# Sliding-window attention in half blocks of 64 queries and 192 keys, on quarter arrays of TensorE

## What is computed

```python
def _alibi_window_bias(diff, key_ok):
    valid = (diff >= 0) & (diff < WINDOW) & key_ok
    slopes = _alibi_slopes()[:, :, None, None]
    pen = -slopes * diff[..., None, None, :, :].astype(jnp.float32)
    return jnp.where(valid[..., None, None, :, :], pen, NEG_BIG)

def _sink_attention(q, k, v, bias, sinks):
    s = jnp.einsum('...qhgd,...khd->...hgqk', q, k).astype(jnp.float32) * (ATT_HEAD_DIM ** -0.5) + bias
    sink = jnp.broadcast_to(sinks.astype(jnp.float32)[:, :, None, None], s.shape[:-1] + (1,))
    p = jax.nn.softmax(jnp.concatenate([s, sink], axis=-1), axis=-1)[..., :-1]
    return jnp.einsum('...hgqk,...khd->...qhgd', p.astype(v.dtype), v)
```

## Time and profile before

| | |
|---|---|
| Runs of the kernel before | 596.15, 596.87, 598.35 us; median 596.87 |
| The profiled execution, its own time | 598.34 us |
| Its span in the profile | 596.5 us |
| Mean granted clock of TensorE over the span | 0.994 |
| Instructions in the profile | 9003 |

### The profile page before, as it was taken

How to read it: one execution, slowest core, us unless ns; L and a number is a source line. 1 busy time by engine, 2 the same in 40 slices (tenths; PEclk the granted TensorE clock), 3 DMA queues, 4 the chain that set the end, 5 groups by cost and what they waited for, 6 DMA issues and landing times.

```text
span 596.5 us, 9003 instructions
## 1 busy us (share of the span) xinstructions
PE 575.7 (97%) x3587; PEld 524.6 (88%) x3587; DVE 272.3 (46%) x536; ACT 208.3 (35%) x548; POOL 138.9 (23%) x145
## 2 busy tenths in 40 slices
PE   4999999998999999999999999999799999999996
PEld 4999999998888888889999898899799998888874
DVE  5620013663666666621376766534345545232323
ACT  6742212414444444430445454223323315021011
POOL 3000031023244334431021312034422221010001
PEclk9999999998999999999999999999999999999998
DMA  9752200621011010013013111411122324134231
GB/s 317 268 186 87 76 1 12 241 78 55 17 37 37 2 36 35 3 36 112 1 44 99 36 56 35 108 36 37 36 71 71 89 88 121 56 141 141 71 123 53
DMA packets 26433, 47.01 MB, mean 79 GB/s; under 512 B 3268, under 2 KB 17860, under 8 KB 26248
## 3 DMA queue, kind: packets, MB, share of 16 engines
q1 hardware_dynamic: 25960, 45.91, 23.7%
q10 hardware_dynamic: 432, 0.53, 0.2%
HBM read 39.40 MB, written 8.01 MB: 79 GB/s over the span
## 4 chain that ended last, share of the span: by engine, by line
PE 88%; ACT 3%; DVE 3%; POOL 3%; issue 2%; DMA 1%; DVEq 0%; ACTq 0%; POOLq 0%
PE ps L547 44%; PE ps L485 8%; PE ps L486 8%; PE ps L487 8%; PE ps L591 3%; PE ps L629 3%; PE ps L611 2%; POOL zaT L1573 2%; PE ps L698 1%; PE ps L732 1%; PE ps L676 1%; PE ps L710 1%; PE ps L490 1%; PE ps L489 1%; PE ps L700 1%
## 5 line engine op out<-in xcount | busy, mean ns | idle before, releaser
L547 PE MATMUL ps<-x_hl,w_hi 128*128 128x364 f32 (+1 forms) x1200 | 305.6, 334 | 12.8 <-ACT x_hl L824 6.5
L547 PEld LDWEIGHTS ps<-x_hl,w_hi 128*128 128x128 f32 x1200 | 212.5, 190 | 22.8 <-issue 7.1
L547 PE MATMUL ps<-x_hl,w_lo 128*128 128x364 f32 (+1 forms) x600 | 199.0, 332 | 0.0
L547 PEld LDWEIGHTS ps<-x_hl,w_lo 128*128 128x128 f32 x600 | 113.8, 190 | 0.1
L940 ACT ACTIVATE prob<-prob,nmx 128x256 f32<-128x256 f32 (+1 forms) x64 | 30.9, 485 | 56.6 <-DVE sd L1239 56.6
L1526 POOL TENSOR_TENSOR prob<-prob,rden 128x1024 f32<-128x1024 f32 (+1 forms) x16 | 28.6, 1789 | 74.2 <-DVE rden L1245 74.2
L328 POOL TENSOR_TENSOR w_lo<-w_raw,w_hi 128x1024 fp32r<-128x1024 f32 x13 | 32.5, 2498 | 47.7 <-ACT w_hi L863 47.7
L485 PE MATMUL ps<-wt_hi,x_hl 128*128 128x324 f32 x128 | 39.9, 312 | 0.0
L487 PE MATMUL ps<-wt_hi,x_hl 128*128 128x324 f32 x128 | 39.8, 311 | 0.0
L486 PE MATMUL ps<-wt_lo,x_hl 128*128 128x324 f32 x128 | 39.8, 311 | 0.0
L1576 POOL TENSOR_TENSOR qmT<-qmT,sg 128x364 f32<-128x364 f32 (+1 forms) x24 | 23.3, 973 | 66.1 <-DVE sg L1428 36.8
(11 more groups left out here) (229 smaller groups left out, 892.8 us busy)
## 6 DMA issues: line engine op xcount, KB each, us to landing
w_raw<-in_w_in_tiles SPq DMA_DIRECT2D x24, 512.0 KB, 3.6
x_tok<-in_x_prompt SPq DMA_DIRECT2D x8, 512.0 KB, 4.5
w_raw<-in_w_out_tiles SPq DMA_DIRECT2D x8, 512.0 KB, 3.6
x_res<-in_x_prompt SPq DMA_DIRECT2D x8, 512.0 KB, 4.1
out_y_prompt<-y_out SPq DMA_DIRECT2D x7, 512.0 KB, 2.9
wt_raw<-in_w_tok SPq DMA_DIRECT2D x4, 648.0 KB, 7.1
Cs<-in_state_C SPq DMA_DIRECT2D x8, 256.0 KB, 2.9
out_C_sample<-Cs SPq DMA_DIRECT2D x8, 256.0 KB, 2.4
```

Source lines behind the costliest of these rows:

```text
L547: last = mm(ps[:, sub_bank(sub), 0:w], wt, xm, start=(at_ == 0), stop=(at_ == 23))
```

## The change

Each block of 128 queries is taken as two halves of 64 (h = 0, 1), and each half meets the 192 keys that end with it. The half's queries lie on one half of the PSUM partitions.

- `scores`: eight products per unit where there were four, each with 64 rows, 64 queries as weights and 192 keys as moving columns. Head kv selects the row half of the array, h the column half.
- The score, exponential and normalising steps run over 192 keys per head instead of 256. Units 0 and 1 run over 128 as before; the first 64 of these have a bias table of their own, `bias_0`.
- `prob_transposes`: for each of four heads one transpose of 128 of its keys, starting at key 0 for g = 0 and at key 64 for g = 1, and for each pair of heads one transpose of the 128 columns that hold the last 64 keys of the one and the first 64 of the other. Six for eight. ACT then copies 256 columns where it copied 512.
- `values`: eight products with 128 keys, then eight with 64, all with 64 queries as moving columns. Group g = 0, 1 writes to bank 4 + g, for every unit, so the unit before must have been copied out: `att_out` is waited for one unit earlier.
- Where a stretch of keys starts in the middle of a token tile, the weights come from `va_sh`, a copy of `va` shifted by 64 tokens, which SP makes by two DMAs from SBUF to SBUF of 64 partitions by 8 tiles by 128 columns (256 KB each). It lies where the raw token-major weights lay.
- The bias table of the prompt has 192 columns per head for 256, and `bias_first` 64.

The core of the diff:

```diff
@@ -205,16 +207,18 @@
-    bias_p = sb("bias_p", [P, AH, 2 * WIN], F32, GI + 17408)
+    bias_p = sb("bias_p", [P, AH, KEYS_H], F32, GI + 17408)
+    bias_0 = sb("bias_0", [P, AH, HQ], F32, GI + 17408 + 4 * AH * KEYS_H)
+    va_sh = sb("va_sh", [P, NC + 1, KV_W], F32, Wr)
...
-    prob = sb("prob", [P, 2, G, 2 * WIN], F32, Fr)
+    prob = sb("prob", [P, 2, G, KEYS_H], F32, Fr)
@@ -390,7 +394,13 @@
+        sp.dma_start(bias_0[:], i["bias_first"]).then_inc(s("att_ld"), 16)
...
+        wait(sp, "wt_lo", 4)
+        wait(sp, "tok_act", NC)
+        wait(sp, "tok_dve", NC)
+        sp.dma_start(va_sh[0:HQ, 1:NC + 1, :], va[HQ:P, 0:NC, :]).then_inc(s("va_sh"), 16)
+        sp.dma_start(va_sh[HQ:P, 0:NC, :], va[0:HQ, 0:NC, :]).then_inc(s("va_sh"), 16)
@@ -584,13 +594,17 @@
             if u < 2 * NC:
                 blk, pair = u // 2, u % 2
-                k0 = 1 if blk == 0 else 0
                 for g in range(2):
-                    for kv in range(KVH):
-                        rows = slice(kv * HD, (kv + 1) * HD)
-                        last = mm(ps[:, kv, g * 256 + k0 * WIN:g * 256 + 256],
-                                  qaT[rows, 2 * pair + g, blk * P:(blk + 1) * P],
-                                  kaT[rows, (blk - 1 + k0) * P:(blk + 1) * P], start=True, stop=True)
+                    for h in range(2):
+                        for kv in range(KVH):
+                            rows = slice(kv * HD, (kv + 1) * HD)
+                            q0 = blk * P + h * HQ
+                            if blk == 0:
+                                keys = kaT[rows, 0:HQ].unsqueeze(1).broadcast_to([HD, 2, HQ]) if h == 0 else kaT[rows, 0:P]
+                            else:
+                                keys = kaT[rows, q0 - WIN:q0 + HQ]
+                            last = mm(ps[h * HQ:(h + 1) * HQ, kv, g * 256 + (HQ if blk == 0 else 0):g * 256 + KEYS_H],
+                                      qaT[rows, 2 * pair + g, q0:q0 + HQ], keys, start=True, stop=True)
             else:
@@ -605,11 +619,17 @@
-            if u < 2 * NC:
-                for kb in range(1 if u < 2 else 0, 2):
-                    for g in range(G):
-                        last = nc.tensor.transpose(ps[:, 2 + kb, g * P:(g + 1) * P],
-                                                   prob[:, u % 2, g, kb * WIN:(kb + 1) * WIN], ident[:])
+            if u < 2:
+                for g in range(G):
+                    last = nc.tensor.transpose(ps[:, 3, g * P:(g + 1) * P], prob[:, u % 2, g, HQ:KEYS_H], ident[:])
+            elif u < 2 * NC:
+                pr = prob[:, u % 2].rearrange("p g k -> p (g k)")
+                for g in range(G):
+                    k0 = KEYS_H * g + HQ * (g % 2)
+                    nc.tensor.transpose(ps[:, 2, g * P:(g + 1) * P], pr[:, k0:k0 + WIN], ident[:])
+                for kv in range(KVH):
+                    k0 = 2 * KEYS_H * kv + WIN
+                    last = nc.tensor.transpose(ps[:, 3, kv * P:(kv + 1) * P], pr[:, k0:k0 + 2 * HQ], ident[:])
             else:
@@ -620,15 +640,37 @@
         def values(u):
...
             wait(pe, "pT_dve", u - 1)
-            wait(pe, "att_out", u - 1)
+            wait(pe, "att_out", u)
             if u < 2 * NC:
...
-                for kb in range(1 if blk == 0 else 0, 2):
-                    for kv in range(KVH):
-                        rows = slice(kv * HD, (kv + 1) * HD)
-                        last = mm(ps[rows, 4 + u % 2, 0:2 * P], va[:, blk - 1 + kb, rows],
-                                  probT[:, u % 2, kb, kv * 2 * P:(kv + 1) * 2 * P],
-                                  start=(kb == 0 or blk == 0), stop=(kb == 1), skip_group_check=True)
+                if u == 0:
+                    pe.wait_ge(s("va_sh"), 32)
+
+                def head(g, rows, h):
+                    return ps[rows, 4 + g, h * HQ:(h + 1) * HQ]
+
+                if blk == 0:
+                    for h in range(2):
+                        for g in range(2):
+                            for kv in range(KVH):
+                                rows = slice(kv * HD, (kv + 1) * HD)
+                                part = slice(0 if h else HQ, P)
+                                last = mm(head(g, rows, h), (va[:, 0, rows] if h else va_sh[HQ:P, 0, rows]),
+                                          probT[part, u % 2, 1, (2 * kv + g) * P + h * HQ:(2 * kv + g) * P + (h + 1) * HQ],
+                                          start=True, stop=True, skip_group_check=True)
+                else:
+                    for g, h in ((0, 0), (0, 1), (1, 0), (1, 1)):
+                        v = va[:, blk - 1 + g] if g == h else va_sh[:, blk]
+                        for kv in range(KVH):
+                            rows, c0 = slice(kv * HD, (kv + 1) * HD), (2 * kv + g) * P + h * HQ
+                            mm(head(g, rows, h), v[:, rows], probT[:, u % 2, 0, c0:c0 + HQ], start=(h == 0), stop=False, skip_group_check=True)
+                    for h in range(2):
+                        for g in range(2):
+                            v = va[:, blk - g] if g == h else va_sh[:, blk + 1 - 2 * g]
+                            for kv in range(KVH):
+                                rows, half = slice(kv * HD, (kv + 1) * HD), slice(g * HQ, (g + 1) * HQ)
+                                last = mm(head(g, rows, h), v[half, rows], probT[half, u % 2, 1, kv * P + h * HQ:kv * P + (h + 1) * HQ],
+                                          start=False, stop=True, skip_group_check=True)
             else:
@@ -944,14 +986,15 @@
-            A_(probT[0:n, u % 2, 1, :], ps[0:n, 3, :], ACT.Copy).then_inc(s("pT_act"), 1)
+            cols = slice(0, 2 * P if 2 <= u < 2 * NC else G * P)
+            A_(probT[0:n, u % 2, 1, cols], ps[0:n, 3, cols], ACT.Copy).then_inc(s("pT_act"), 1)
...
         def out_evac(u):
...
             if u < 2 * NC:
                 blk, pair = u // 2, u % 2
...
-                   ps[:, 4 + u % 2, 0:2 * P].rearrange("p (g t) -> p g t", g=2), ACT.Copy)\
+                   ps[:, 4:6, 0:P], ACT.Copy)\
...
             else:
@@ -1217,14 +1260,17 @@
-                dve.wait_ge(s("att_ld"), 64)
+                dve.wait_ge(s("att_ld"), 80)
...
             if u < 2 * NC:
...
-                k0 = WIN if u < 2 else 0
-                p = prob[:, b, :, k0:]
-                step(STT(out=p, in0=ps[:, 0:2, :].rearrange("p b (g k) -> p (b g) k", g=2)[:, :, k0:], scalar=rstd_q[:, u // 2:u // 2 + 1],
-                         in1=bias_p[:, heads, k0:], op0=ALU.mult, op1=ALU.add))
+                p = prob[:, b, :, HQ if u < 2 else 0:]
+                raw = ps[:, 0:2, :].rearrange("p b (g k) -> p (b g) k", g=2)
+                parts = [(0, KEYS_H, bias_p)] if u >= 2 else [(HQ, WIN, bias_0), (WIN, KEYS_H, bias_p)]
+                for k0, k1, bias in parts:
+                    last = STT(out=prob[:, b, :, k0:k1], in0=raw[:, :, k0:k1], scalar=rstd_q[:, u // 2:u // 2 + 1],
+                               in1=bias[:, heads, :] if bias is bias_0 else bias[:, heads, k0:k1], op0=ALU.mult, op1=ALU.add)
+                step(last)
...
             else:
@@ -1605,8 +1651,9 @@
-    diff = tok[:, None, None] + WIN - np.arange(2 * WIN)[None, None, :]
+    diff = tok[:, None, None] % HQ + WIN - np.arange(KEYS_H)[None, None, :]
...
+    bias_first = np.where(tok[:, None, None] < HQ, f(NEG), bias_prompt[:, :, HQ:WIN])
```

More of the change, by code:

```diff
@@ L43 @@
 KEYS_S = WIN + DEC_T
+HQ = P // 2
+KEYS_H = WIN + HQ
 W1 = MD + 1
@@ L215, in build @@
     prob_s = sb("prob_s", [P, 4, KEYS_S], F32, Fr)
-    new_s = sb("new_s", [P, 4, T_S], F32, Fr + 2560)
-    k_out = sb("k_out", [P, 2, KV_W], F32, Fr + 4096)
+    new_s = sb("new_s", [P, 4, T_S], F32, Fr + 6144)
+    k_out = sb("k_out", [P, 2, KV_W], F32, Fr + 7168)
     mx = small("mx", [P, 2, 4])
@@ L936, in exps @@
             b = u % 2
-            k0 = WIN if u < 2 else 0
+            k0 = HQ if u < 2 else 0
             for g in range(4):
@@ L980, in g_exp @@
                 act.wait_ge(s("v_out"), 32)
-                act.wait_ge(s("att_ld"), 64)
+                act.wait_ge(s("att_ld"), 80)
                 A_(Gt[:, 0, 0:2, :].rearrange("p h t -> p (h t)"), ps[:, 0, 256:512], ACT.Exp).then_inc(s("g_done"), 1)
@@ L1523, in normalise @@
             if u < 2 * NC:
-                k0 = WIN if u < 2 else 0
+                k0 = HQ if u < 2 else 0
                 p = prob[:, b, :, k0:]
-                Q.tensor_tensor(p, p, rden[:, b, :].unsqueeze(2).broadcast_to([P, G, 2 * WIN - k0]), ALU.mult)\
+                Q.tensor_tensor(p, p, rden[:, b, :].unsqueeze(2).broadcast_to([P, G, KEYS_H - k0]), ALU.mult)\
                     .then_inc(s("prob_ready"), 1)
@@ L1626, in constants @@
             "seq_mask": np.where(same & (st[:, None] <= st[None, :]), f(-NEG), f(NEG)),
-            "bias_prompt": bias_prompt, "bias_sample": bias_sample, "resets": resets,
+            "bias_prompt": bias_prompt, "bias_first": bias_first, "bias_sample": bias_sample, "resets": resets,
```

## The result

| | before | change |
|---|---|---|
| Median of 7 runs each | 598.35 us | 592.94 us |
| Lowest and highest | 596.15, 598.53 | 589.86, 594.56 |
| Profiled execution | 598.34 us | 594.56 us |
| Its mean granted clock | 0.994 | 0.992 |

The ratio is 0.9912 (0.9886 to 0.9938), 5.4 us less on the medians. The forecast was 589.6 us, in a range from 587.0 to 594.0. The change is faster by more than 0.5%, by 5.4 us on the medians where 7.3 were forecast, about three quarters, and its runs are spread over 4.7 us. The forecast of 589.6 started from a median of 596.87 for the kernel before; in this comparison that median was 598.35, and the same -7.3 us counted from it gives 591.1.

What follows compares the result with a forecast made beforehand. PE's own work was taken to set the time in the attention stretches. Terms -9.0 (units 2 to 15), +0.3 (units 0 and 1) and +1.4 (DMA queue) sum to -7.3 us: 589.6 us from a median of 596.87, range 587.0 to 594.0.

Steps and rivals of the forecast that it cites:

- Attention blocks, -9.0 + 0.3: PE's transposes, values and scores: 0.64 us less in each of units 2 to 15, 0.3 more for units 0 and 1.
- Rival 4: Scores and second values, units 2 to 15: quarter arrays run only two at a time; +4.9 us, 601.8; chance 0.04.
- rival 5: PE's short value rounds pay on top of their columns, 0.086 for 0.058 us; 4.7 us, 594.3; chance 0.03.
- Unit 0's values: Values of units 0 and 1: four rounds on quarters and four on halves, 0.76 us, 0.18 more each.
- the join: Second values to scores on PE, units 2 to 15: no gap; gain 9.0 us with it, 6.8 without.
- Rival 2: No join: pipe empties between second values and scores, 14 x 0.16 = 2.2 us; 591.8, or 593.5 with the clock; chance 0.15.
- Other engines, nothing: Attention stage: shorter score, exponential, POOL and ACT copy work costed at nothing, since PE hides it.
- The DMA queue, +1.4: SP's two shifted copies ahead of weight tile 4 delay its landing and PE near 122 us: 512 KB at 371 GB/s.
- The upper bound, 2.8: DMA delay of weight tile 4 by the shifted copies: 2.8 us if read and write cost both.
- PE pays each further delay in full: PE's start on weight tile 4 near 122 us: every further delay of its landing delays PE equally, +1.4 us.
- The clock, rival 1: The longer wait at 122 us, 0.7 to 2.1, also drops PE's clock: 1.7 us, 591.3; chance 0.25.
- The forecast case: Whole kernel: all terms as summed, -7.3 us, 589.6 us against the median; chance 0.45.

Runs made afterwards that it cites:

- parts_swapped: Changed kernel with its value parts in the other order, 64-key products first, 128-key products second: 591.36 us, ratio 0.99.
- before_copies: Kernel before plus only the change's two SBUF-to-SBUF copies at the same place of SP's queue, data unused: 599.71 us, ratio 1.0034.
- tile4_first: Changed kernel with weight tile 4 loaded ahead of all attention loads and the shifted copies issued behind it: 589.52 us, ratio 0.9865.
- before_dram: Kernel before plus one unused 512 KB load from HBM in the place of the two SBUF-to-SBUF copies: 596.85 us, ratio 0.999.
- change_rows_early: Changed kernel, copies still ahead of tile 4, with exponentials of the gate rows made one sub-block earlier: 587.13 us, ratio 0.9814.
- the second: Second comparison: the changed kernel unaltered, run once more against the kernel before: 590.27 us, ratio 0.9891.
- copies_late: Changed kernel with its two shifted copies issued behind the load of weight tile 4, not ahead of the window copies: 588.84 us, ratio 0.9859.
- copies_late_again: copies_late run once more, unaltered, beside a rerun of the changed kernel: 590.32 us, ratio 0.9871.
- rows_early_first: tile4_first with exponentials of the gate rows made one sub-block earlier: 585.70 us, ratio 0.9802.
- rows_early_late: copies_late with exponentials of the gate rows made one sub-block earlier: 586.52 us, ratio 0.9815.

## Why the prediction was right and where it was wrong

**Attention blocks, -9.0 + 0.3: right to a twentieth.** 8.24 us measured for 8.7. Each of the four blocks is within 0.01 of its term. Two roads led there: counting from start to start, and reading the sample's blocks as prices for small tiles. Rival 4 (pairs) is refuted by the same rows, sixteen score records in 0.76 us where it asked for 1.41, and so is rival 5 (0.086 a round), by value parts of 0.62 and 0.28 where it asked for 0.83 and 0.39. The Trainium skill (TensorEngine Tiling, Instruction Overhead) gives each matmul some 60 cycles of overhead. As something added to each it does not show here: without their borders the first value part and the scores leave rounds of 0.059 and 0.164, for columns that need 0.054 and 0.161. Unit 0's values are also as summed, 159.91 to 160.67, 0.76.

**What is missing of it is the join, counted 14 times.** It needs values followed by scores of the prompt. PE's timeline at the last such place:

```profile
244.77 0.27 PE L672 MATMUL ps<-probT,va 64*64 64x64 f32 x2
...
245.17 0.69 PE L614 MATMUL ps<-kcT,qs 64*32 64x136 f32 x32
```

Here the second part takes 0.40 for 0.28, and the last two units are followed by a projection. Eleven units join, three pay, 3 x 0.16 = 0.5 us. The loop quoted ahead of the prediction says so (`if it < N_ATT`); I had taken a middle unit for all. Rival 2 itself did not come: in the change no gap stands between 64x64 blocks that meet, and parts_swapped shows the gap coming back at its forecast price.

**Other engines, nothing: right.** No wait of PE for probabilities or copies stands in the waits of the change.

**The DMA queue, +1.4: the term that failed.** I named the right transfer and the right engine. Two halves of the step were wrong. The price: "512 KB at 371 GB/s" took bytes for bytes, but the landing moved by 3.35 in the profiled execution, by 2.9 in before_copies, and by 0.9 for the same bytes from memory. The upper bound, 2.8 if read and write cost both, came nearer in the first two, though other executions of the copies show 1.7 and about 2. And "PE pays each further delay in full" was false in the other direction. POOL's 3.56 us of the earlier trace rows was not the split's own length. DVE's timeline of the kernel before in those microseconds, and POOL's in tile4_first, where it began together with another of DVE's scans:

```profile
118.26 2.25 DVE L1188 TENSOR_TENSOR_SCAN row<-row,row 4x1024 f32<-4x1024 f32 x1
120.45 3.25 DVE L1191 TENSOR_TENSOR_SCAN row<-row,m0T,row 4x8 f32<-4x8 f32 x8
```

```profile
115.92 2.39 POOL L332 TENSOR_TENSOR w_lo<-w_raw,w_hi 128x1024 fp32r<-128x1024 f32 x1 [10.79 <-ACT w_hi L905]
```

Unhindered the split takes 2.4. In the kernel before it stood behind DVE's scan until 120.4 and ended at 122.71. A tile that ACT can begin by about 119.2 (its 1.1 us, then POOL at 120.4) costs PE nothing, which before_dram shows; each microsecond after that costs one. Two traces bear this out: with landings of 119.70 (change_rows_early) and 120.91 (before_copies), 0.5 and 1.7 past that point, PE waits 1.01 and 2.21, which is 0.46 and 1.66 more than 0.55. In the change's first profile the landing at 121.36 leaves 2.16, and 0.67 come on top, since POOL's split (3.06 for 2.39) now met another row of DVE, the first of these two:

```profile
122.06 1.28 DVE L1242 TENSOR_TENSOR rows<-row,row 4x1088 f32<-4x1088 f32 x1
123.38 3.31 DVE L1243 TENSOR_TENSOR rows<-row,row 4x1088 f32<-4x1088 f32 x1
```

That makes the 2.83.

**The clock, rival 1, given 0.25: it came in both profiled executions of the change,** for 1.61 us at 125.69. Other executions were probably without it, though none of them was profiled: 594.71 less the 2.37 between waits of 3.38 and 1.01 and less two falls of 1.6 is 589.1, and 589.3 is the lowest that was measured. My reason against it, that 0.7 us of wait dropped nothing, was sound for 0.7 and said little of a wait whose length I had sized too small.

**The sum.** Forecast -8.7 + 1.4 = -7.3. In the profiled execution: -8.24 + 2.83 + 1.61 = -3.80. Over the runs the two last terms vary: -5.4 by the medians of the first comparison and -7.5 by those of the second (597.78 to 590.27). The forecast case is one that the change has in some executions and not in others. That the first median fell inside the range owes something to luck. The upper end of 594.0 was made of rivals 1 and 2. Rival 2 did not come, and its 2.2 us made room for a DMA term larger than summed and for a median of the kernel before that was 1.5 us higher; the profiled execution, 594.56, lies outside.

**Open:** why tile 4 lands at 119.7 in one execution and 121.7 in another with the same queue (the DMA records show the difference already in the window copies ahead of it, which end at 117.93 and 119.86); and what decides, after the same 2.2 us of waiting, whether the granted clock falls. One part of the change was not tried by itself, the second bias table.

## What to carry to other kernels

Count a saving at every place where it is made, the first and last rounds of a loop apart: a border between two blocks is there only where the two blocks meet. Before a kernel's new copies are priced, look at what stands behind them in the same queue and at what it must beat: here the order of a few lines cost up to 4.4 us in an execution, of the 8.2 that the change gains in its blocks, and with the gate rows early, putting the urgent load ahead of everything gave another 0.8 (585.70 for 586.52). A wait of PE of 2.2 us cost 3.8 here in some executions, by the fall of the clock after it; taking it away made the kernel faster and its times narrower, so that smaller effects can be measured at all.

## What was not expected of the hardware

**POOL and DVE held each other up.** In tile4_first POOL's split and a DVE scan began 0.05 us apart; POOL took its 2.39 and the scan 4.60 for 2.41:

```profile
115.97 4.60 DVE L1230 TENSOR_TENSOR_SCAN row<-resets,row 4x1088 f32<-4x1088 f32 x1
```

4.60 is the sum of the two less 0.2. In copies_late the scan came first and it was POOL that waited:

```profile
118.67 4.25 POOL L332 TENSOR_TENSOR w_lo<-w_raw,w_hi 128x1024 fp32r<-128x1024 f32 x1 [13.38 <-ACT w_hi L905]
```

DVE's eight small scans took 1.16 in the change and 3.25 in the kernel before, and in the change a product of 4 partitions took 3.31 for 1.28 (the two rows of DVE above). The Trainium skill (SBUF — State Buffer, Terms) says that the two engines share a pair of ports whose lock is held for a whole instruction, and that the loser "fully blocks"; these rows agree, with instructions of four partitions on one side. A long row of POOL or DVE beside the other's is thus no measure of its own length.

**Two copies from SBUF to SBUF weighed more than one load of the same bytes:** ahead of tile 4 512 KB moved its landing by 0.9 us from memory, in one trace, and by between 1.7 and 3.7 from SBUF, in five (119.70 to 121.67, against 118.01; without either it came between 117.53 and 118.57).

**The granted clock fell after the same wait in some executions and not in others.** After the wait of 2.22 us before scores(0) the stretch took 4.80 us at a granted 1.00 or 6.3 at 0.73, that is partly at 1.2 GHz for 2.4, in kernels that differ in nothing there: copies_late 4.80 above, and copies_late_again, the same program:

```profile
138.81:145.10 6.29, 6.29 (x40) 5.92 (x40) 2.30 (x8) 2.69 (x10) 1.18 (x2) 0.73 0.04 11
```

It fits the two levels of the kernel before, near 596.8 and 598.4: the profile at 598.34 has the fall, and that of before_dram at 596.70 has none. Of the nine traces with this wait six show the fall. After tile 4 it came after both waits of 3.38 and after none of 0.55, 1.01, 1.34 and 2.21.

A fall can also cost nothing. After another wait of PE, of 2.17 us near 409, the clock fell in rows_early_first and not in rows_early_late:

```profile
408.40:413.00 4.60, 4.60 (x18) 4.60 (x19) 1.73 (x2) 2.71 (x4) 1.60 (x2) 0.63 0.01 4
```

```profile
408.40:413.00 4.60, 3.92 (x23) 3.93 (x24) 2.36 (x4) 2.03 (x4) 0.98 (x1) 1.00 0.02 4
```

Yet rows_early_first is the faster of the two by 0.71 us (585.67 and 586.38 in the profiled executions), as much as its lead when that wait ended (408.39 against 409.07): PE at full clock waited again, 1.12 us at 418.43 and 0.20 at 422.89, and the slower PE did not. So a fall of the clock cost time where PE's own work set the time afterwards, and not here.
